# A hybrid decoder layer: the input projection multiplies x without the norm's root, which goes to the results, with a new order of loads and of VectorE's work

## What is computed

```python
def rms_norm(x, g):
    y = x * lax.rsqrt(jnp.mean(x * x, axis=-1, keepdims=True) + RMS_EPS)
    return y * g

h = rms_norm(x, norm_pre_mix)
proj = h @ w_in                                     # 1024 x (256 + 1032 + 1024 + 768)
u_s5, p_ml, p_rw, p_mb = split_cols(proj, ...)
y = concat([s5_mixer(u_s5), mlstm_mixer(p_ml), rwkv7_mixer(p_rw), moba_mixer(p_mb)])
x = x + rms_norm(rms_norm_per_group(y) @ w_out, norm_post_mix)
x = x + rms_norm(cross_attention(rms_norm(x, g1), rms_norm(mem, g2)), g3)
x = x + rms_norm(swiglu(rms_norm(x, g4)), g5)
```

## Time and profile before

| | us |
|---|---|
| median of 3 runs (520.61 to 520.7) | 520.66 |
| the profiled execution | 520.58 |
| its span, first instruction to last | 518.8 |
| TensorE busy | 487.5 |
| VectorE busy | 378.5 |
| ScalarE busy | 261.8 |
| GpSimd busy | 167.0 |

### The profile page before, as it was taken

The page is one execution under the profiler, slowest core; times in us unless marked ns, Lnnn a source line. Parts: engine busy times, 40 slices in busy tenths (PEclk is TensorE's granted clock), DMA queues, the critical chain, the costliest instruction groups (busy, mean ns, idle before and its releaser), DMA issues.

```text
span 518.8 us, 8480 instructions
## 1 busy us (share of the span) xinstructions
PE 487.5 (94%) x3494; PEld 446.7 (86%) x3494; DVE 378.5 (73%) x445; ACT 261.8 (50%) x412; POOL 167.0 (32%) x101
## 2 busy tenths in 40 slices
PE   0799999979999999999999999999999999999985
PEld 0789889978899878878999988999999999988874
DVE  5676797997756889587756466699999999962114
ACT  3598864412622334666856557544445444443333
POOL 0040227297669360000000000244334433443540
PEclk9999999989999999999999999999999999999999
DMA  8937328022031222626373460275445555545502
GB/s 334 375 96 233 150 81 322 3 82 81 1 100 64 82 82 81 244 82 220 120 270 125 155 223 26 82 265 183 163 167 195 205 173 200 199 162 198 208 1 81
DMA packets 12358, 79.33 MB, mean 153 GB/s; under 512 B 1440, under 2 KB 2080, under 8 KB 3488
## 3 DMA queue, kind: packets, MB, share of 16 engines
q1 hardware_dynamic: 12320, 78.79, 42.5%
HBM read 76.95 MB, written 1.84 MB: 152 GB/s over the span
## 4 chain that ended last, share of the span: by engine, by line
PE 84%; DVE 8%; ACT 3%; issue 2%; DMA 1%; POOLq 0%; POOL 0%; SPq 0%; DVEq 0%; ACTq 0%
PE bank L381 82%; DMA ring<-weights 1%; DVE arena L1668 1%; ACT w_high L356 1%; DVE vx L1695 1%; DVE arena L1485 1%; POOLq L90 0%; POOL w_rest L362 0%; DVE arena L1660 0%; DVE we_rest L362 0%; DVE arena L1661 0%; DVE wk_rest L362 0%; DVE arena L1839 0%; DVE wm_rest L362 0%; PE bank L814 0%
## 5 line engine op out<-in xcount | busy, mean ns | idle before, releaser
L362 POOL TENSOR_TENSOR w_rest<-ring,w_high 128x1024 fp32r<-128x1024 f32 x21 | 50.8, 2418 | 202.6 <-ACT w_high L356 202.6
L356 ACT ACTIVATE w_high<-ring 128x1024 fp32r<-128x1024 f32 x66 | 69.4, 1058 | 72.7 <-PE bank L381 72.6
L381 PE MATMUL bank<-h_high,w_high 128*128 128x256 f32 x384 | 102.9, 283 | 0.0
L381 PE MATMUL bank<-h_rest,w_high 128*128 128x256 f32 x352 | 99.6, 283 | 0.0
L381 PE MATMUL bank<-h_high,w_rest 128*128 128x256 f32 x320 | 90.6, 283 | 0.0
L362 DVE TENSOR_TENSOR w_rest<-ring,w_high 128x1024 fp32r<-128x1024 f32 x39 | 49.8, 1282 | 37.4 <-ACT w_high L356 37.4
L381 PEld LDWEIGHTS bank<-h_high,w_high 128*128 128x128 f32 x384 | 71.7, 192 | 0.5 <-issue 0.4
L381 PEld LDWEIGHTS bank<-h_rest,w_high 128*128 128x128 f32 x352 | 67.6, 192 | 0.0
L381 PE MATMUL bank<-arena 128*128 128x128 f32 (+7 forms) x496 | 59.2, 300 | 6.5 <-DVE arena L1691 4.5
L381 PEld LDWEIGHTS bank<-arena 128*128 128x128 f32 (+3 forms) x496 | 52.8, 182 | 12.6 <-DVE arena L1691 5.1
L381 PEld LDWEIGHTS bank<-h_high,w_rest 128*128 128x128 f32 x320 | 61.4, 192 | 0.0
(11 more groups left out here) (323 smaller groups left out, 1230.6 us busy)
## 6 DMA issues: line engine op xcount, KB each, us to landing
ring<-weights SPq DMA_DIRECT2D x50, 1024.0 KB, 5.0
third_slot<-weights SPq DMA_DIRECT2D x15, 1024.0 KB, 5.1
cst<-consts SPq DMA_DIRECT2D x1, 1664.0 KB, 12.6
gain<-gains SPq DMA_DIRECT2D x3, 512.0 KB, 5.8
par<-params SPq DMA_DIRECT2D x1, 1168.0 KB, 14.9
kx<-x_t SPq DMA_DIRECT2D x1, 1024.0 KB, 4.9
vx<-mem_t SPq DMA_DIRECT2D x1, 1024.0 KB, 10.3
xres<-x_rows SPq DMA_DIRECT2D x1, 1024.0 KB, 10.4
```

Of the source, the lines that this page charges most:

```text
L356: nc.scalar.activation(split_half(i)[0], raw_half(i), ACT.Copy).then_inc(S["w_high"], 1)
L362: e.tensor_tensor(rest_, raw_half(i), high.bitcast(F32), ALU.subtract).then_inc(rest_done(i)[0], 1)
L381: return nc.tensor.matmul(out_, lhsT, rhs, start=start, stop=stop, skip_group_check=True)
```

## The change

- Loads: first parameters, the bias masks (`onehot`, 33 rows, now at the front of the constants), x in two halves with the two halves of slot 0 between and behind, slot 1, ones and eps; the other constants behind slot 2, the other parameters behind slot 3, mem behind slot 4.
- h's parts are made of x times gain, without the root: `x_high` and `x_rest`, tile by tile. The sum of squares follows later, inside `rw_k`. The root goes to the results: VectorE multiplies eight banks by it in place (`x_scale`), evacuates `s5_u` and `mb_k` with it (`project_scaled`); token-major values (`ml_v`, `mb_v`) get it as a scale per partition (`project_values` with `rstd_col`), MoBA's q through `q_col` in the scores. `w_gate` is multiplied by the gain.
- The bias products come first on TensorE; `rw_g` gets bank 4, `rw_r` bank 3; mem's sum moves behind `ml_q`.
- S5's phases go from ScalarE to VectorE; both Sin behind the tanh of `rw_w` and `rw_a`.
- `level_update(1)` ahead of `rests(H_MID + 4)` and `scan(0)`; `scan(1)` behind mLSTM's masks; on GpSimd the third level mask ahead of `rotate_back(0)`.
- `solution(1)` ahead of S5's sigmoid; `gn_s5` one step later; the last two halves go to two buffers that are free.

The diff, cut to its core:

```diff
 def split_half(i):
+            if i >= NHALF - 2:
+                return (w_kx, w_wo[0])[i - NHALF + 2]
 def high_part(act, i):
-            if i % 2 == 0:
+            if i == 0:
+                act.wait_ge(S["half0_in"], 16)
+            elif i % 2 == 0 or i == 1:
                 wait_slot(act, i // 2)
-            if before >= start:
+            if before >= start and i < NHALF - 2:
+        SCALED = ["rw_wag", "rw_k", "rw_r", "rw_v", "ml_q", "ml_k", "gates", "ml_o"]
+        def scaled(eng, name):
+            eng.wait_ge(S["x_scaled"], SCALED.index(name) + 1)
+            return bank[uses[name][0]]
@@ program of TensorE @@
-            o = pe_open(pe, "x_sumsq", 0)
-            pe.wait_ge(S["x_summed"], 4)
-            mm(o[:, 0:T], const("ones"), sq_x[:, 0, :]).then_inc(full[0], 1)
-            split_channel_major(0, "rw_wag", 1, h_split, lambda j: pe.wait_ge(S["h_rest"], j + 1))
-            split_channel_major(1, "rw_k", 0, h_split)
             for h in range(NH):
                 o = pe_open(pe, f"rel{h}", 4 + h)
...
+            split_channel_major(0, "rw_wag", 1, h_split, lambda j: pe.wait_ge(S["h_rest"], j + 1))
+            split_channel_major(1, "rw_k", 0, h_split, None, (0,))
+            o = pe_open(pe, "x_sumsq", 2)
+            pe.wait_ge(S["ones_in"], 16)
+            pe.wait_ge(S["x_summed"], 3)
+            mm(o[:, 0:T], const("ones"), sq_x[:, 0, :])
+            for m in range(2):
+                last = mm(o[:, T + m:T + m + 1], sq_x[:, 0, m * P:(m + 1) * P], const("ones")[:, 0:1])
+            last.then_inc(full[2], 1)
+            split_channel_major(1, "rw_k", 0, h_split, None, (1,))
-                if kt == 0:
+                if kt == 1:
                     group_sumsq("gn_s5", 0, 3)
@@ program of GpSimd @@
-            rotate_back(0)
             level_mask(3)
+            rotate_back(0)
@@ program of ScalarE @@
+            for k in range(4):
+                x_high(k)
+            highs(1)
+            act.wait_ge(S["x_high_in"], 16)
+            for k in range(4, KD):
+                x_high(k)
             highs(2)
+            x_square(0)
             highs(4)
+            x_square(1)
             a.activation(step, prm("log_step"), ACT.Exp).then_inc(S["s5_step"], 1)
...
+            highs(6)
+            o = wait_full(act, "x_sumsq")
+            a.activation(rstd_col, o[:, T:T + 2], ACT.Ln, bias=const("eps6"), scale=1.0 / D)
+            inv_root("x_sumsq", rstd_x, T, 1.0 / D, "eps6").then_inc(S["rstd_x"], 1)
+            a.activation(rstd_col, rstd_col, ACT.Exp, scale=-0.5).then_inc(S["rstd_col"], 1)
             shifted("rw_wag", 0)
+            highs(7)
             shifted("rw_k", 1)
             highs(8)
@@ program of VectorE @@
+            for k in range(4):
+                x_rest(k)
+            rests(1)
+            dve.wait_ge(S["x_high_in"], 16)
+            for k in range(4, KD):
+                x_rest(k)
+            rests(4)
+            dve.wait_ge(S["sq_ready"], 2)
+            sum_tiles(dve, v, sq_x, "x_summed")
+            rests(6)
+            x_scale("rw_wag")
+            for i in range(8):
+                last = v.tensor_scalar(sin[:, i, :], const("time"), frac[:, i:i + 1], None, ALU.mult)
+            x_scale("rw_k")
             mix(0, "rw_wag")
+            rests(7)
+            for i in range(8):
+                last = v.tensor_scalar(cos[:, i, :], const("time"), frac[:, i:i + 1], ROUND, ALU.mult, ALU.add)
             mix(1, "rw_k")
             rests(8)
+            x_scale("rw_r")
...
-            scan(0)
-            rests(H_MID + 4)
+            rests(H_MID + 3)
             level_update(1)
+            rests(H_MID + 4)
+            scan(0)
...
+            solution(1)
+            rests(H_WKV + 11)
             dve.wait_ge(S["s5_exp"], 1)
             sigmoid_of_exp(z5b, "s5_sig", 0).then_inc(S["s5_sig"], 1)
-            rests(H_WKV + 11)
-            solution(1)
```

More of the change, by code:

```diff
@@ L609, in _ @@
                 last = mm(o[:, j, :], prm("g2")[:, j * P:(j + 1) * P], rwE[:, 0, 1, :])
-            last.then_inc(full[2], 1)
+            last.then_inc(full[4], 1)
             split_channel_major(5, "ml_q", 0, h_split)
+            o = pe_open(pe, "mem_sumsq", 7)
+            pe.wait_ge(S["mem_summed"], 3)
+            mm(o[:, 0:T], const("ones"), sq_m[:, 0, :]).then_inc(full[7], 1)
             o = pe_open(pe, "rw_kk", 3)
@@ L1571, in _ @@
             mix(2, "rw_r")
+            x_scale("rw_v")
             rests(10)
@@ L1638, in _ @@
             rests(16)
+            x_scale("ml_k")
+            rests(17)
             conv_back(1, "ml_k")
-            rests(17)
+            x_scale("gates", GATES, 1)
             dve.wait_ge(S["rw_k2"], 3)
@@ L1724, in _ @@
             rests(H_MID + 6)
-            scan(1)
+            project_scaled("mb_k", mqk[:, 2:4, :])
             moved(dve, "g_col")
```

175 lines of the change are left out of this document (88 added, 87 removed).

## The result

The changed kernel takes 512.0 us (median of four executions, 511.39 to 514.33) beside 520.68 for the kernel before: ratio 0.983, 95% interval 0.982 to 0.985. A second job gave 511.84 and 0.982 (0.981 to 0.984). The forecast was 504.6, its range 500.0 to 510.5: the sign was right, and 8.7 of the 16.0 us came. The profiled execution took 511.39 with a span of 509.6, 9.2 less than before.

A forecast was written before the change was run, and what follows sets the result against it. TensorE, busy 94% of the span, was taken as the bound, leaving its idle and half-paced time to win, with VectorE limiting the start. 7.3 + 5.0 + 1.3 + 0.7 + 1.7 = 16.0 us off 520.6 gave 504.6, range 500.0 to 510.5.

The forecast's parts named there:

- The first product: Start: the first weight product no longer needs the root and starts at about 9.2 instead of 16.84, 7.6 us earlier.
- Rival (c): Start: half transfers bring nothing, half 0 still lands at 9.2, first product at 11.8, 2 us lost: 506.6; chance 0.15.
- Pace of the first 22 matmuls: Start: bias products in front bring TensorE to full pace, saving 2.0 us; 33 rows might not raise it.
- TensorE's side: Start: earlier product, moved bias products, pace and rw_g's own bank could bring TensorE alone 12.4 us earlier at ml_o's end.
- VectorE's side: Start: with 10.4 us of added work and 3 us of remaining idle time, VectorE reaches the A masks 7.3 us earlier.
- The loop at `ml_k`: Before the A masks: ml_k's scaling is followed by ScalarE's conv_now, only then the next high part; 1.8 us idle on VectorE.
- Rival (b): Start: phases and scalings cost double beside GpSimd and VectorE bounds: 517, half of it 511; chance 0.16 for 508 or more.
- Level update: Level stage: level_update(1) ahead of scan 0 removes TensorE's 3.96 us gap and 1.3 of half pace; 5.0 us gained.
- It just fits: Level stage: rotate_back(0), behind scan 0 and GpSimd's third mask, is ready for its product 12 us after the gap.
- Later orders: Later stages: solution(1) ahead of the sigmoid gains 1.3 us, gn_s5 a step later 0.7, free buffers for the last halves 1.7.
- scan 0's read-out: Level stage, a sign that the forecast is wrong: scan 0's read-out starts to hold TensorE.
- The two other signs: Start, signs of a wrong forecast: TensorE's waits before 77 sum to over 5 us, or phases take over 0.5 each.

The follow-up runs named there:

- gap_filled: Changed kernel with the bias products on 128 rows and three more such products, results unused, behind the four to fill TensorE's wait; 513.51 us, 0.985.
- rows_before_update: Changed kernel with ml_k's scaling first, gate rows ahead of level_update(1), mem's norm behind level_update(2), rotate_back(0) ahead of the third mask; 513.83 us, 0.986.
- level_split_rows: Changed kernel with ml_k's scaling first, level_update(2) in the middle of the gate rows, rotate_back(0) ahead of the third mask; 511.76 us, 0.983.
- front_reordered: level_split_rows with the front reordered: scalings one step earlier, phases later, big constants and parameters each a slot later; 512.31 us, 0.983.
- level_waits_filled: Changed kernel with ml_k's scaling first, plus 6 and 14 unused TensorE products ahead of S5's first read-out and the third level product; 509.95 us, 0.981.
- mask4_split: level_split_rows with GpSimd's fourth level mask moved ahead of rotate_back(1); 509.45 us, 0.978.

## Why the prediction was wrong

**The first product** (forecast 9.2, came at 10.09). x's lower half was placed at 5.0 by proportion from the old landing; ScalarE started on it at 6.12, so the high part of the first half slot started at 7.73, where my sum has 6.6. Rival (c), that half transfers bring nothing, didn't happen.

**Pace of the first 22 matmuls** (term 2.0 of TensorE's side). Wrong as a fact, by the case that I named: with 33 rows the pace didn't rise, and with 128 it rose but was lost in the wait of 2.06 that followed. `gap_filled` shows that the term was worth nothing anyway.

**VectorE's side** (7.3, came 5.1 at the first A mask). The work was sized right: from the end of S5's decay at 19.2 to 79.49, less 4.3 us of idle time, are 56.0 us, and the forecast had 59.2 - 3.0 = 56.2. Phases took 0.27 each (0.30 assumed); scalings stand 0.61 apart, as assumed. It failed by the start, 19.2 instead of 18.1, which is the late first product again, and by the idle time, 4.3 instead of 3.0: 1.4 more for the root, which my walk didn't have. The loop at `ml_k`, put at 1.8, came as 1.85. Rival (b) in its mechanism didn't happen; that its half priced 511 is chance.

**Level update** (5.0, came 0.0 net in the ledger, 1.1 to 1.7 against the kernel with the order undone). This is the step that failed. The gap and the half pace that I subtracted did go, 5.1 us. "It just fits" and "it fits too" were said of GpSimd's steps without walking what they wait for. I took scan 0 as early as the rest. It ended 1.9 us later than before. VectorE was 5.1 earlier at the A masks and 4.6 earlier at mem's norm; then two rest parts and an update now stand in front of the scan (4.7 us, from 95.65 to 100.31), and two of its four scans ran beside GpSimd's mask, 1.58 and 1.52 us instead of 0.66. On that chain, scan 0, `rotate_back(0)`, `rotate(1)`, scan 1, `rotate_back(1)`, hangs the fourth level mask, whose halves came 1.4 and 0.4 us earlier than before while TensorE came 7.0 earlier. The mask's own 4.12 us have a part in this: it started 2.3 earlier than before. The stage took back all of the 5.1: 3.3 with the waits at 110 and 113, 1.4 at the fourth level product, 0.4 at 179. Three variants removed the first two waits (`rows_before_update`, `level_split_rows`, `front_reordered`); they met the last one at 6.70, 2.44 and 3.95. A gain in front that doesn't bring scan 0 forward as well can pass this product only by what the mask has in hand.

**Later orders** (1.3, 0.7, 1.7; 3.7 in sum) came as 1.3, 0.9 and 1.8, 4.0 in sum, and two runs confirm them by their traces.

**Sum.** 2.1 in front (TensorE's 5.2 for 7.3) and 5.0 in the level stage, less 0.3 that the later orders gave more, and 0.5 between the medians and the profiled executions are the missing 7.3. My range was too narrow because all its cases varied the front: none let the level stage give back what it won, though I had named scan 0's read-out as a thing that would make me wrong. The two other signs stayed out: TensorE's waits before 77 sum to 4.9 with the one ahead of the first weight product, and the phases took 0.27 each.

## What to carry to other kernels

When work is moved ahead of a step on an in-order engine, follow the step that was passed, with its new start, through every engine that hangs on it until the chain rejoins the critical engine; the 4.4 us that the fourth mask had in hand were used up by a gain of 7. Make that walk before adding savings of two stages: the sum can't exceed what the slowest chain allows. And an edit that burdens the busier engine can pay, as the phases did, when it clears the queue through which the evacuations pass. And compare two variants by when the critical engine reaches the same instruction, not by medians alone: two of the differences here (3.9 and 1.7 us) shrank to 1.8 and 1.1 that way.

## What the runs showed of the hardware

- 33-row products at full issue, eight records in 5.46 us, stayed at 0.64 a record, the pace of 1.2 GHz; 128-row ones of the same length went over to 0.32, at 7.41, before they were done. Why the rows matter isn't settled by these two runs.
- After the wait of 2.06 us that followed, matmuls started 0.213 apart; after one of 0.35 they started 0.12 apart. The clock column says 1.00 at the start in all of them; only the spacing tells. The length of a wait alone doesn't decide: after 2.17 us (`gap_filled`) and 2.44 (`level_split_rows`) they came at half pace, after 2.02 (`level_waits_filled`) and 2.62 (`mask4_split`) at full pace.
- A VectorE scan that starts while a GpSimd operation runs waits for that operation. Two 128x256 scans took 1.58 and 1.52 us beside GpSimd's mask and 0.66 each without it. A 4x256 scan took 1.66 and in some places 0.68 to 0.71, so few rows make it no cheaper. What decides is the start:

```profile
104.57 1.39 POOL L1047 TENSOR_TENSOR arena<-arena 128x512 f32<-128x512 f32 x1 [1.79 <-DVE arena L1732]
104.83 1.66 DVE L1781 TENSOR_TENSOR_SCAN arena<-cst,arena 4x256 f32<-4x256 f32 x1
```

  GpSimd's operation ends at 105.96, the scan at 106.49. From 85 on, in the traces of all twenty runs, 69 scans of 256 columns started while a GpSimd operation was running, and all 69 ended 0.5 to 0.6 us behind its end; the 291 others took 0.66 to 0.69. The 0.68 in `rows_before_update` started at 90.32, 0.04 ahead of GpSimd's mask. Eight operations of the norm took 9.64, 4.92 and 4.00 us in three places. The Trainium skill (GPSIMD Engine Reference, Key points) says that GpSimd shares its SBUF interfaces with VectorE and collides with its instructions that read two SBUF tensors. These scans read two, and the traces agree.
- The granted clock fell to 0.72 over 6 us in some executions with hardly any idle time of TensorE in the stretch, as in the first of the two windows above. A wait of 1.08 had ended just ahead of that one; `mask4_split` has the same wait (1.07) and kept 1.00.
